# VectorE takes over TensorE's transposes of the heads' outputs, the spatial weights and the per-layer input

## The reference

```python
z = rms_norm(h, attn_norm_g) @ w_in                    # q, k, v, u, g
attn = probs[:, :, 0] - lam * probs[:, :, 1]           # four heads, two maps each
o_diff = rms_norm(einsum('bhqk,bkhe->bqhe', attn, v), subln_g) * (1.0 - lam_init)
vn = layer_norm(gelu(zg))                              # eight groups of 128
s = einsum('gij,bnjgc->bnigc', where(mask, ws, 0), vn) + bs
o_gmlp = gelu(zu) * s
h = h + concatenate([o_diff, o_gmlp]) @ w_out
h = h + (silu(f @ w1) * (f @ w3)) @ w2
h = h + (p @ pl_w_up) * sigmoid(h @ pl_w_gate)
```

## Time and profile before

| | |
|---|---|
| median of 3 runs | 2619.94 us |
| profiled execution, its own time | 2619.69 us |
| its span | 2617.9 us |
| TensorE (PE) busy | 2609.1 us, 100% |
| VectorE (DVE) busy | 1600.7 us, 61% |
| ScalarE (ACT) busy | 1169.3 us, 45% |
| DMA traffic | 503.43 MB, 192 GB/s |

### The profile page before, as it was taken

One profiled execution on the slowest core, in us unless ns is written; L12 is line 12 of the kernel. 1 busy time (PEld: TensorE's weight loads), 2 busy tenths in 40 slices (PEclk: granted clock), 3 DMA queues, 4 the chain that ended last, 5 costly groups with the idle time before them and its releaser, 6 DMA issues.

```text
span 2617.9 us, 50695 instructions
## 1 busy us (share of the span) xinstructions
PE 2609.1 (100%) x21361; PEld 2547.9 (97%) x21361; DVE 1600.7 (61%) x1646; ACT 1169.3 (45%) x1259; POOL 14.6 (1%) x33
## 2 busy tenths in 40 slices
PE   9999999999999999999999999999999999999998
PEld 8989999999999999999999999999999989998997
DVE  6568765555555556795676666556777655555555
ACT  5346544434443444465443333444544434443444
POOL 2000000000000000000000000000000000000000
PEclk9999999999999999999999999999999999999999
DMA  9644556555555555566555555655565555555553
GB/s 306 193 161 157 198 194 193 192 193 193 192 192 194 192 194 193 178 202 199 178 191 191 182 191 182 199 187 197 195 211 195 194 193 190 192 196 193 191 194 130
DMA packets 253254, 503.43 MB, mean 192 GB/s; under 512 B 8334, under 2 KB 10400, under 8 KB 252976
## 3 DMA queue, kind: packets, MB, share of 16 engines
q1 hardware_dynamic: 250160, 496.27, 57.2%
q10 hardware_dynamic: 1952, 3.68, 0.4%
q0 software_dynamic: 992, 1.34, 0.2%
HBM read 498.37 MB, written 2.88 MB: 191 GB/s over the span
## 4 chain that ended last, share of the span: by engine, by line
PE 100%; DVE 0%; ACT 0%; POOL 0%; issue 0%; DVEq 0%; POOLq 0%
PE ps L1457 49%; PE ps L1468 25%; PE ps L1494 4%; PE ps L1496 4%; PE ps L1495 4%; PE ps L1515 4%; PE ps L1524 4%; PE ps L1519 3%; PE ps L1504 1%; PE ps L1505 1%; PE ps L1502 1%; PE ps L1410 0%; PE ps L1417 0%; PE ps L1658 0%; PE ps L1656 0%; PE ps L1657 0%
## 5 line engine op out<-in xcount | busy, mean ns | idle before, releaser
L883 DVE TENSOR_TENSOR lo<-raw,hi 128x1024 fp32r<-128x1024 f32 x939 | 1143.2, 1224 | 882.4 <-ACT hi L545 868.6
L545 ACT ACTIVATE hi<-raw 128x1024 fp32r<-128x1024 f32 x939 | 990.7, 1060 | 1245.4 <-PE ps L1468 943.8
L1457 PE MATMUL ps<-A,hi 128*128 128x256 f32 x7283 | 903.2, 276 | 0.0
L1457 PEld LDWEIGHTS ps<-A,hi 128*128 128x128 f32 x7283 | 861.0, 188 | 0.3
L1457 PE MATMUL ps<-B,hi 128*128 128x256 f32 x3961 | 491.3, 276 | 0.0
L1468 PE MATMUL ps<-A,lo 128*128 128x256 f32 x3648 | 487.6, 276 | 0.0
L1457 PEld LDWEIGHTS ps<-B,hi 128*128 128x128 f32 x3961 | 468.2, 188 | 0.1
L1468 PEld LDWEIGHTS ps<-A,lo 128*128 128x128 f32 x3648 | 447.3, 188 | 0.0
L1468 PE MATMUL ps<-B,lo 128*128 128x256 f32 x1984 | 265.2, 276 | 0.0
L1468 PEld LDWEIGHTS ps<-B,lo 128*128 128x128 f32 x1984 | 243.3, 188 | 0.0
L1495 PE MATMUL ps<-lo,B 128*128 128x512 f32 x336 | 130.7, 389 | 0.0
(11 more groups left out here) (265 smaller groups left out, 1231.2 us busy)
## 6 DMA issues: line engine op xcount, KB each, us to landing
raw<-in_w_in_dram SPq DMA_DIRECT2D x135, 1024.0 KB, 5.2
raw<-in_ffn_w_dram SPq DMA_DIRECT2D x132, 1024.0 KB, 5.1
raw<-in_w_gate_up_dram SPq DMA_DIRECT2D x88, 1024.0 KB, 5.0
raw<-in_w_down_dram SPq DMA_DIRECT2D x44, 1024.0 KB, 5.0
raw<-in_w_out_dram SPq DMA_DIRECT2D x16, 1024.0 KB, 5.1
raw<-in_pl_w_gate_dram SPq DMA_DIRECT2D x16, 1024.0 KB, 5.0
raw<-in_conv_out_w_dram SPq DMA_DIRECT2D x16, 1024.0 KB, 5.0
raw<-in_w_o_dram SPq DMA_DIRECT2D x16, 1024.0 KB, 5.0
```

Of the source, the lines that this page charges most:

```text
L545: act.activation(hi[:, slot % RING], raw[:, raw_slot, 2 * (slot % 2):2 * (slot % 2) + 2, :], ACT.Copy).then_inc(hi_ready, 1)
L883: dve.tensor_tensor(lo[:, slot % RING], raw[:, slot // 2 % RAWS, 2 * (slot % 2):2 * (slot % 2) + 2, :], hi[:, slot % RING], ALU.subtract). ...
L1457: pe.matmul(ps[:, b0 + m, 0:T], high(slot, kk, m), x, start=j == 0 and kk == 0 and part == 0, stop=False)
```

## The change

VectorE's transpose works on blocks of 32 by 32, so a 128x128 transpose is put together from blocks that are read from one group of 32 partitions and written to another.

- `turn_out` becomes `turn_o0`, `turn_o1` and `out_parts`, one and two pieces after `head_norm` and then at the old place: sixteen VectorE transposes of 32 partitions by 128 elements per head, into `o_turned` in SBUF, from which ScalarE and VectorE then write the two parts.
- The spatial weights are transposed by twelve VectorE instructions of 32 by 256 in `ws_turn0` to `ws_turn3`, spread over pieces 3, 4, 5 and 7 of qk; their transposes on TensorE and the copy out of PSUM go.
- Their row sums are made by two VectorE reductions at piece 2 of qk; ScalarE writes them to HBM in single elements of 4 bytes, reads them back at piece 10 of qk as a row for all partitions, and `ws_bias` waits for that in place of TensorE.
- `turn_p` uses sixteen VectorE transposes of 32 by 128 in place of four on TensorE.

```diff
-    ("v", 13): ["ws_out"], ("v", 15): ["read_bias"], ("qk", 1): ["lambda"], ("qk", 6): ["mask_bias"], ("out", 9): ["meta_squares"],
-    ("g", 2): ["ws_sums"], ("g", 3): ["ws_bias"], ("u", 10): ["spatial0"], ("u", 12): ["spatial1"],
+    ("v", 13): ["ws_out"], ("v", 15): ["read_bias"], ("qk", 1): ["lambda"], ("qk", 2): ["ws_sums"], ("qk", 3): ["ws_turn0"],
+    ("qk", 4): ["ws_turn1"], ("qk", 5): ["ws_turn2"], ("qk", 6): ["mask_bias"], ("qk", 7): ["ws_turn3"], ("qk", 10): ["read_sums"], ("out", 9): ["meta_squares"],
+    ("g", 3): ["ws_bias"], ("u", 10): ["spatial0"], ("u", 12): ["spatial1"],
...
-    for _step, _at in (("scores", 0), ("turn", 4), ("pv", 6), ("head_norm", 7), ("turn_out", 10)):
+    for _step, _at in (("scores", 0), ("turn", 4), ("pv", 6), ("head_norm", 7), ("turn_o0", 8), ("turn_o1", 9), ("out_parts", 10)):
...
-        o_head = work[:, 0:2, :]
+        o_head, o_turned = work[:, 0:2, :], work[:, 2:4, :]
...
+        row_sums = nc.dram_tensor("gate_row_sums", [8, P], F32, kind="Internal").ap()
...
+        p_turned = work[:, 0:2, :]
+        ws_total = ln_stats[:, 0:8]
...
+                elif step in ("ws_turn0", "ws_turn1", "ws_turn2", "ws_turn3"):
+                    pass
+                elif step == "ws_sums":
+                    asked.skip()
+                    wait(asked)
+                    act.dma_start(row_sums[:, :].rearrange("g i -> i g"), ws_total, allow_slow_non_contiguous=True).then_inc(sums_written, 16)
+                elif step == "read_sums":
+                    act.wait_ge(sums_written, 16)
+                    act.dma_start(pb_copy[:, :, :].rearrange("p k t -> p (k t)"),
+                                  row_sums[:, :].rearrange("g i -> (g i)").unsqueeze(0).to_broadcast([P, 1024])).then_inc(sums_landed, 16)
...
                 elif step == "turn_p":
-                    pe_out.skip()
-                    wait(pe_out)
-                    act.activation(PT[:, :, 0:T], ps[:, 4 * ((G + 1) % 2), :].rearrange("p (k t) -> p k t", k=2), ACT.Copy).then_inc(to_dve, 1)
-                    given.skip()
+                    asked.skip()
+                    wait(asked)
+                    given.mark(act.activation(PT[:, :, 0:T], p_turned, ACT.Copy))
...
-                    elif name == "turn_out":
-                        pe_out.skip()
-                        wait(pe_out)
+                    elif name in ("turn_o0", "turn_o1"):
+                        pass
+                    elif name == "out_parts":
+                        asked.skip()
+                        wait(asked)
                         for i in range(2):
-                            last = act.activation(B_high[:, 2 * hd + i, :], ps[:, 6, i * T:(i + 1) * T], ACT.Copy, scale=small[:, 20 + i:21 + i])
+                            last = act.activation(B_high[:, 2 * hd + i, :], o_turned[:, i, :], ACT.Copy, scale=small[:, 20 + i:21 + i])
                         given.mark(last)
...
-                    step(dve.tensor_copy(wsT[:, :, :], ps[:, 2:4, :].rearrange("p b (g i) -> p (b g) i", i=P)))
-                    step(dve.memset(wsT[CHUNK:P, :, 0:CHUNK], 0.0))
...
                 elif what == "ws_sums":
-                    pe_out.skip()
+                    step(dve.tensor_reduce(ws_total[0:CHUNK, :], ws_in[0:CHUNK, :, 0:CHUNK], AXX, ALU.add))
+                    hand(dve.tensor_reduce(ws_total[CHUNK:P, :], ws_in[CHUNK:P, :, :], AXX, ALU.add))
+                elif what in ("ws_turn0", "ws_turn1", "ws_turn2", "ws_turn3"):
+                    r = int(what[-1])
+                    to = slice(32 * r, 32 * r + 32)
+                    if r == 0:
+                        step(dve.memset(wsT[CHUNK:P, :, 0:CHUNK], 0.0))
+                    for q in range(4):
+                        if r < 2 or q >= 2:
+                            last = dve.transpose(wsT[to, :, 32 * q:32 * q + 32], ws_in[32 * q:32 * q + 32, :, to])
+                    step(last)
                 elif what == "ws_bias":
-                    dve.wait_ge(pe_done, pe_out.now())
+                    dve.wait_ge(sums_landed, 16)
                     dve.wait_ge(late_landed, 16)
                     for g in range(8):
-                        last = dve.scalar_tensor_tensor(out=bs_row[:, g, :], in0=ps[:, 6 + g // 4, (g % 4) * P:(g % 4 + 1) * P],
+                        last = dve.scalar_tensor_tensor(out=bs_row[:, g, :], in0=pb_copy[:, g // 2, (g % 2) * P:(g % 2 + 1) * P],
...
-                    pe_out.skip()
+                    dve.wait_ge(p_landed, 16)
+                    by_k = p_turned.rearrange("p k (a c) -> p k a c", c=P)
+                    for q in range(4):
+                        for r in range(4):
+                            x = p_in[32 * q:32 * q + 32, :, :].rearrange("p a (k c) -> p k a c", c=P)
+                            last = dve.transpose(by_k[32 * r:32 * r + 32, :, :, 32 * q:32 * q + 32], x[:, :, :, 32 * r:32 * r + 32])
+                    hand(last)
                     given.skip()
                     wait(given)
-                    pe_in.mark(dve.tensor_tensor(PT[:, :, T:2 * T], ps[:, 4 * ((G + 1) % 2), :].rearrange("p (k t) -> p k t", k=2),
-                                                 PT[:, :, 0:T], ALU.subtract))
+                    pe_in.mark(dve.tensor_tensor(PT[:, :, T:2 * T], p_turned, PT[:, :, 0:T], ALU.subtract))
...
-                        pe_in.mark(last)
-                    elif name == "turn_out":
-                        pe_out.skip()
+                        own.mark(last)
+                        wait(own)
+                    elif name in ("turn_o0", "turn_o1"):
+                        by_e = o_turned.rearrange("p e (a c) -> p e a c", c=P)
+                        for q in range(4)[:2] if name == "turn_o0" else range(4)[2:]:
+                            for r in range(4):
+                                x = o_head[32 * q:32 * q + 32, :, :].rearrange("p a (e c) -> p e a c", c=P)
+                                last = dve.transpose(by_e[32 * r:32 * r + 32, :, :, 32 * q:32 * q + 32], x[:, :, :, 32 * r:32 * r + 32])
+                        if name == "turn_o1":
+                            hand(last)
+                    elif name == "out_parts":
                         given.skip()
                         wait(given)
                         for i in range(2):
-                            last = dve.scalar_tensor_tensor(out=B_low[:, 2 * hd + i, :], in0=ps[:, 6, i * T:(i + 1) * T],
+                            last = dve.scalar_tensor_tensor(out=B_low[:, 2 * hd + i, :], in0=o_turned[:, i, :],
...
-                    for g in range(8):
-                        pe.transpose(ps[:, 2 + g // 4, (g % 4) * P:(g % 4 + 1) * P], ws_in[:, g, :], ident[:, :])
...
-                elif what == "ws_sums":
-                    for c in range(2):
-                        last = pe.matmul(ps[:, 6 + c, :], ones[:, :], wsT[:, 4 * c:4 * c + 4, :], start=True, stop=True)
-                    done.mark(last)
...
-                    pe.wait_ge(p_landed, 16)
-                    pe.wait_ge(psum_free, G)
-                    for k in range(2):
-                        for a in range(2):
-                            last = pe.transpose(ps[:, 4 * ((G + 1) % 2), k * T + a * P:k * T + (a + 1) * P], p_in[:, a, k * P:(k + 1) * P], ident[:, :])
-                    done.mark(last)
...
-                    elif name == "head_norm":
-                        v_in.skip()
-                    elif name == "turn_out":
-                        wait(v_in)
-                        for e in range(2):
-                            for a in range(2):
-                                last = pe.transpose(ps[:, 6, e * T + a * P:e * T + (a + 1) * P], o_head[:, a, e * P:(e + 1) * P], ident[:, :])
-                        done.mark(last)
+                    elif name in ("head_norm", "turn_o0", "turn_o1", "out_parts"):
+                        pass
```

More of the change, by code:

```diff
@@ L176 @@
 for _head in range(HEADS):
-    for _step, _at in (("scores", 0), ("turn", 4), ("pv", 6), ("head_norm", 7), ("turn_out", 10)):
+    for _step, _at in (("scores", 0), ("turn", 4), ("pv", 6), ("head_norm", 7), ("turn_o0", 8), ("turn_o1", 9), ("out_parts", 10)):
         _n = 1 + 6 * _head + _at
         SIDE.setdefault(("g", _n) if _n < 16 else ("u", _n - 16), []).append((_step, _head))
-SIDE[("u", 0)] = ["norm_stats"]
+SIDE[("u", 0)].append("norm_stats")
 SIDE[("u", 1)].append("norm_root")
-SIDE[("u", 5)] = ["norm_scale"]
+SIDE[("u", 5)].append("norm_scale")
 SIDE.setdefault(("u", 14), []).append("gate_mix0")
@@ L319, in bass_two_blocks @@
             sem("first_raw_piece_landed"), sem("first_half_piece_hi"), sem("first_half_piece_lo"), sem("first_x_low"))
+        sums_written, sums_landed = sem("sums_written"), sem("sums_landed")
         skew_written, bias_landed, late_landed, stored = (
@@ L723, in side @@
                     pass
-                elif step in ("ws_sums", "spatial0", "spatial1"):
+                elif step in ("spatial0", "spatial1"):
                     pe_out.skip()
```

(14 more changed lines are left out.)

## The result

The changed kernel takes 2629.81 us (median of 5 runs, 2629.64 to 2632.73) against 2619.89 of the kernel before beside it: ratio 1.0041, 95% interval 1.003 to 1.0051, so 0.4% slower. The forecast was 2625.8 us.

A forecast was written before the change was run, and what follows sets the result against it. TensorE, busy 2609.1 of 2617.9 us, was taken as the bound. Stall +6.2, TensorE work removed behind it -0.88 and p's block +0.5 gave +5.8 us: 2625.5 profiled, 2625.8 median; range 2621.2 to 2630.5.

The forecast's parts named there:

- the 4.79 us off TensorE: TensorE's queue: row sums 1.71, four heads 1.76, p 0.44 and spatial weights 0.88 us leave it.
- Price of a transpose: VectorE: 299 ns per 32x128 transpose, 0.316 us each from start to start, no overlap; eight with entry 2.60 us.
- qk: Weights' transposes, reductions and memset add at most nine us to VectorE, hidden in 9.1 idle us; cost taken as nothing.
- head 0: Its two halves, 5.2 us on VectorE before head 1's scores, mostly fill 4.99 idle us; 0.3 us stay.
- The stall: Four halves between the evacuations of g and u put u's evacuation and then `pv` 6.2 us later.
- TensorE's idle time: TensorE should stand idle for 5.8 + 4.8 = 10.6 us.
- TensorE comes out of its gaps slowly: Rival: two long gaps before a piece of u and `pv` cost 3.5 us more, 2629.3 us; chance 0.18.
- After it two items: Behind `pv`, head 3's and p's transposes leave TensorE, -0.88 us; p's VectorE block in out adds 0.5.
- the full price: Rival: each VectorE transpose costs the full 0.453 us, 3.70 a half, giving 2635 us; chance 0.06.

The follow-up runs named there:

- experiment 3: The changed kernel with all four heads and p transposed on TensorE again, leaving only the weights' transposes and row sums on VectorE: 2617.24 us, ratio 0.999.
- experiment 9: The changed kernel with all four heads back on TensorE; weights, row sums and p stay on VectorE: 2616.8 us, ratio 0.9988 to the kernel before.
- experiment 10: The changed kernel with heads 1 to 3 back on TensorE; head 0, weights, row sums and p stay on VectorE: 2617.21 us.
- Experiment 2: The changed kernel with heads 1 and 2 back on TensorE; heads 0 and 3, weights, row sums and p stay on VectorE: 2621.24 us.
- experiment 1: The changed kernel plus four unread 128x128 identity transposes on TensorE at u 13, where head 3's transposes stood before: 2627.53 us.
- experiment 5: The changed kernel with head 1 alone transposed on TensorE again: 2628.5 us.
- experiment 6: The kernel before with all four heads' outputs transposed by VectorE; weights, row sums and p as before: 2631.78 us.
- Experiment 4: The kernel before with only head 3's output and p transposed by VectorE: 2623.48 us, ratio 1.0013.
- experiment 7: The kernel of Experiment 2 plus one unread 128x128 identity transpose on TensorE at u 13: 2617.36 us, ratio 0.9992 to the kernel before.

## Why the prediction was wrong, step by step

- **Who is the bound, and the 4.79 us off TensorE: right.** Experiments 3 and 9 gain 2.7 and 3.0 us, for the 2.59 and 3.03 of the parts they hold. But the premise that every us out of TensorE's queue is a us of the kernel does not hold for all of it (last point).
- **Price of a transpose: right.** 303 ns for 299. Eight last 2.50 to 2.53 us, the next instruction starts 2.52 to 2.56 behind the first, for 2.60. (The 0.08 for going into them should be 0.10 by its own rows, 3.52 - 3 x 1.14.) They don't overlap. The rule of the Trainium skill, "VectorE: DVE Perf Modes", section "Two Vector instructions with no wait between them", that an output in another group of 32 partitions holds an instruction says the same; the trace agrees, with 0.315 us from one to the next.
- **qk: right, and head 0 as far as the kernel after shows.** No wait in qk, where VectorE goes from 12.79 to 17.58 busy us of 21.90. g is evacuated at 199.79, 1.95 earlier than before (forecast 2.2). By itself head 0 on VectorE gains nothing (experiment 10 against 9).
- **The stall: right in place and size.** u evacuated at 233.08 (forecast 232.9), GELU behind 9.95 idle us, `pv` at 236.61 (236.5). Experiment 2 shows that heads 1 and 2 make it. One name is off: this `pv` is the fourth of the trace, head 3's at piece 9 of u, and not head 2's, as the rows, the prediction and the expectations have it; the parts and the probabilities that ScalarE writes ahead of it are those of heads 2 and 3. The times and the sum are not touched by it.
- **TensorE's idle time: 6.0 us, not 10.6.** 2.4 of the difference is the half-clock piece, which counts as busy. The rest was not followed up.
- **The rival "TensorE comes out of its gaps slowly" was right on the mechanism, but it is not what made this trace longer.** The Trainium skill, "TensorE: Matmul & The Clock Gate", Part 1, has the clock fall when the engine idles; here it falls to 0.50, the 1.2 GHz level, behind a wait of 3.03 us. Its forecast of 2629.3 lies near the result by accident, and so does the upper part of the range, to 2630.5, which was set for it: the kernel after pays for no half clock that its trace shows. Experiments 1, 5 and 6 do pay, because there it falls behind `pv`. The scatter of the kernel after (2631.3 and 2632.73 in two of five runs) may be the same; that was not seen.
- **The step that failed: "After it two items: head 3's transposes and those of p leave TensorE, -0.88 ... I take 0.5 (bounds 0 and 3.2, the latter at the full price)".** The -0.88 is right as work, and the 0.5 is 0: p's block makes TensorE wait nowhere in out, and experiment 9 lies 0.44 below experiment 3 (0.3 if each is taken against the kernel before beside it). What was missing is that head 3's transposes ended a slow pace of TensorE (with head 3 alone removed, p's end it, experiment 6). Removing all eight costs 4.4 us: 6.3 - 0.9 + 0 + 4.4 = 9.8 of the 9.9 between the spans. Experiment 4 shows it alone: -0.88 + 4.4 = +3.5 us. The bounds were bounds for VectorE; none was set for removed TensorE work costing more than it took. The rows to see it by were in the trace of before: steps of 0.118 ahead of head 3's transposes, of 0.113 behind them.

What puts TensorE into the slow pace stays open. In all twelve traces it follows the second spatial block, and no run changed that block. Shorter slow stretches stand elsewhere in u, such as 196.07 to 201.73 and 223.74 to 226.10 after, and 212.96 to 223.68 in experiment 1. One of them ends at a wait of TensorE (226.10, the 3.03 us), others at the probabilities' transposes, which elsewhere stand ahead of a slow stretch (223.74), so the kind of instruction alone doesn't tell.

One thing in the kernel bears on this that neither the prediction nor the experiments took into account. At some pieces the tables behind `steps_of` (FIRST_TURN and EVERY_TURN) have one matmul of 256 columns issued as two, in the places named here of 128 columns each. Further on in the trace of before a slow stretch of 27 steps ends at such a split (L1455): eight low-half matmuls take 0.94 us ahead of it (1178.53 to 1179.47) and 0.90 behind (1181.42 to 1182.32).

```profile
1178.53 1.10 PE L1468 MATMUL ps<-B,lo 128*128 128x256 f32 x8
1179.47 0.64 PE L1457 MATMUL ps<-B,hi 128*128 128x256 f32 x4
1179.94 0.33 PE L1455 MATMUL ps<-B,hi 128*128 128x128 f32 x2
...
1181.42 1.07 PE L1468 MATMUL ps<-B,lo 128*128 128x256 f32 x8
1182.32 1.98 PE L1457 MATMUL ps<-B,hi 128*128 128x256 f32 x16
```

The same stretch ends the same way in all twelve traces. So transposes are not the only thing that ends the pace. The first spatial block has a split right behind it (piece 11 of u), and the quick pace follows in eleven of the twelve traces (in experiment 7 the pace was slow ahead of the block and stayed so); the second has none behind it, and the slow pace follows in all twelve. Whether a split at piece 13 of u would do what head 3's transposes did, no run shows.

## What to carry to other kernels

Where one engine is busy all the time, work taken off it is a gain only if the engine that takes it over has room in that very stage: p's four transposes were worth 0.3 to 0.4 us in out, head 0's four nothing in g, and those of heads 1 and 2 cost 6 us between two evacuations. Before removing small instructions from a long uniform row, compare the step from start to start ahead of them and behind them; what looks like overhead may be what restores the pace. And a late start is charged twice only if the engine's slow restart falls behind its last wait.

## What the runs showed of the hardware

- TensorE has two paces for the same 128x256 matmul at a granted clock of 1.00: 0.113 and 0.118 us from start to start. It stayed in the slow one for up to 119 us without a wait (after, 250.02 to 368.63), and one 128x128 transpose in u brought it out within 0.7 us (experiment 7), as did a 256-column matmul issued as two halves (before, 1179.94). The Trainium skill, "TensorE: Matmul & The Clock Gate", section "Back-to-back issue gap", gives N/2.4 + 2.5 ns for an isolated matmul, an estimate of 109 ns for 256 columns, and for a stream with weight loads some 131 ns at 512 columns. The rows have two steps at 256, and 0.23 us at 512, and the rows decide.
- TensorE's waits of 2.7 to 4.2 us in u (after, experiments 1, 5 and 6) were each followed by 3 to 6 us at half pace, a step of 0.21 instead of 0.113 at a granted clock near 0.5; behind one of 1.3 us (experiment 5, 226.42) the step was back at 0.113 after three matmuls.
- Eight transposes of 32x128 (fp32) on VectorE take 2.51 us, 0.315 from one to the next; 303 ns each, 436 for 32x256.
